# Weight products whose moving columns are read, and whose bank columns are written, from last to first

## The reference

```
h = rmsnorm(x); proj = h @ w_in          # 2048 x (512 + 4*768 + 12 + 2*768)
mixed = concat(pool_mixer, gated_deltanet, rglru_mixer)
x = x + mixed @ w_out                    # 2048 x 2048
x = x + (gelu(dwconv(gate)) * val) @ w_down   # gate, val = split(rmsnorm(x) @ w_up), 2 x 6144 wide
x = rmsnorm(x)
```

```
u = rmsnorm(x) @ w_in_2                  # 2048 x D_IN: latents, heads of three branches, gates
o_a, o_b, o_c = latent, difference and banded attention (8 heads each)
y = sum over n: sigmoid(gate_n) * ((o_n * silu(z_n)) @ w_branch[n])
x = x + y @ w_out_2
```

## Time and profile before

| | |
|---|---|
| median of three runs | 3365.55 us (3365.45 to 3366.45) |
| span of the profiled execution, first to last instruction | 3364.8 us |
| matmuls, of which in L191 to L193 and L205 to L207 | 27834, 24384 |
| busy: TensorE, VectorE, ScalarE, GpSimd | 3322.3, 2191.7, 1711.6, 309.8 us |
| HBM | 580 MB read, 173 GB/s over the span |

### The profile page before, as it was taken

How to read it: one execution, slowest core, us unless ns; L and a number is a source line. 1 busy time by engine, 2 the same in 40 slices (tenths; PEclk the granted TensorE clock), 3 DMA queues, 4 the chain that set the end, 5 groups by cost and what they waited for, 6 DMA issues and landing times. The chain is left out here.

```text
span 3364.8 us, 72970 instructions
## 1 busy us (share of the span) xinstructions
PE 3322.3 (99%) x27834; PEld 3282.9 (98%) x27834; DVE 2191.7 (65%) x3584; ACT 1711.6 (51%) x2803; POOL 309.8 (9%) x314
## 2 busy tenths in 40 slices
PE   8999999999999999999999999999999999999999
PEld 7999999999999998899999999999899999999999
DVE  7667666656656666678755665665778755666655
ACT  5555644434434455656544554444665654554443
POOL 1010100000000025011002200001012101210000
PEclk9999999999999999999999999999999999999999
DMA  5234555555555554444455545555444455445554
GB/s 190 107 112 148 176 186 189 189 186 187 188 187 187 187 187 159 139 163 158 161 197 184 183 161 188 188 201 177 146 153 163 156 178 209 172 162 188 187 206 162
DMA packets 90629, 584.28 MB, mean 174 GB/s; under 512 B 10480, under 2 KB 11120, under 8 KB 28400
## 3 DMA queue, kind: packets, MB, share of 16 engines
q1 hardware_dynamic: 88992, 577.47, 48.7%
q0 software_dynamic: 1488, 4.72, 0.4%
HBM read 580.05 MB, written 2.10 MB: 173 GB/s over the span
## 5 line engine op out<-in xcount | busy, mean ns | idle before, releaser
L172 DVE TENSOR_TENSOR w_lo<-raw,w_hi 128x768 fp32r<-128x768 f32 (+5 forms) x1202 | 1378.5, 1159 | 372.6 <-ACT w_hi L161 365.6
L191 PE MATMUL bank<-h,w_hi 128*128 128x256 f32 x5168 | 1459.3, 282 | 16.5 <-DVE w_lo L172 12.0
L161 ACT ACTIVATE w_hi<-raw 128x768 fp32r<-128x768 f32 (+4 forms) x1190 | 1095.7, 968 | 692.3 <-PE bank L193 615.4
L193 PE MATMUL bank<-h,w_lo 128*128 128x256 f32 x5168 | 1444.1, 279 | 0.0
L192 PE MATMUL bank<-h,w_hi 128*128 128x256 f32 x5168 | 1443.6, 279 | 0.0
L191 PEld LDWEIGHTS bank<-h,w_hi 128*128 128x128 f32 x5168 | 973.1, 188 | 22.0 <-DVE w_lo L172 10.2
L192 PEld LDWEIGHTS bank<-h,w_hi 128*128 128x128 f32 x5168 | 973.2, 188 | 2.6 <-issue 1.9
L193 PEld LDWEIGHTS bank<-h,w_lo 128*128 128x128 f32 x5168 | 972.8, 188 | 0.0
L191 PE MATMUL bank<-mixed,w_hi 128*128 128x256 f32 x2272 | 634.9, 279 | 0.7 <-DVE w_lo L172 0.7
L193 PE MATMUL bank<-mixed,w_lo 128*128 128x256 f32 x2272 | 634.5, 279 | 0.0
L192 PE MATMUL bank<-mixed,w_hi 128*128 128x256 f32 x2272 | 633.8, 279 | 0.0
(11 more groups left out here) (408 smaller groups left out, 3340.4 us busy)
## 6 DMA issues: line engine op xcount, KB each, us to landing
raw<-in_w SPq DMA_DIRECT2D x485, 1024.0 KB, 4.8
raw<-in_w_br SPq DMA_DIRECT2D x96, 512.0 KB, 3.8
raw<-in_w_uq SPq DMA_DIRECT2D x8, 768.0 KB, 4.4
raw<-in_w_ukv SPq DMA_DIRECT2D x8, 512.0 KB, 3.3
bias_t<-in_bias POOLq DMA_DIRECT2D x16, 192.0 KB, 4.2
x<-in_x SPq DMA_DIRECT2D x4, 512.0 KB, 7.7
raw<-in_w_kr SPq DMA_DIRECT2D x4, 512.0 KB, 3.3
out_x<-x SPq DMA_DIRECT2D x3, 512.0 KB, 7.5
```

What stands on the lines that cost most here:

```text
L161: act.activation(w_hi[:, b % 2, c], raw[:, b, c], ACT.Copy).then_inc(S["hi_done"], 1)
L172: dve.tensor_tensor(w_lo[:, b % 2, c], raw[:, b, c], w_hi[:, b % 2, c].bitcast(F32), ALU.subtract).then_inc(S["lo_done"], 1)
L191: pe.matmul(o, w_hi[:, b % 2, c], a_hi, start=start and k == t0, stop=False)
L193: last = pe.matmul(o, w_lo[:, b % 2, c], a_hi, start=False, stop=stop and k == t0 + nt - 1)
```

## The change

The three matmuls of each tile get the moving operand and the output as views whose columns run backwards. Both are reversed, so the result of each column lands in the column where it was. The stationary tiles, the readers of the banks and all other matmuls stay as they are.

```diff
+        def back(v):
+
+            return v[:, ::-1]
+
         def unit(pe, n, b, act_of, outs, ready=None):
...
-                    pe.matmul(o, w_hi[:, b % 2, c], a_hi, start=start and k == t0, stop=False)
-                    pe.matmul(o, w_hi[:, b % 2, c], a_lo, start=False, stop=False)
-                    last = pe.matmul(o, w_lo[:, b % 2, c], a_hi, start=False, stop=stop and k == t0 + nt - 1)
+                    pe.matmul(back(o), w_hi[:, b % 2, c], back(a_hi), start=start and k == t0, stop=False)
+                    pe.matmul(back(o), w_hi[:, b % 2, c], back(a_lo), start=False, stop=False)
+                    last = pe.matmul(back(o), w_lo[:, b % 2, c], back(a_hi), start=False, stop=stop and k == t0 + nt - 1)
...
         def unit_tiles(pe, n, b, act_of, o, k0, k1, ready=None):
...
-                pe.matmul(o, w_hi[:, b % 2, c], a_hi, start=k == 0, stop=False)
-                pe.matmul(o, w_hi[:, b % 2, c], a_lo, start=False, stop=False)
-                last = pe.matmul(o, w_lo[:, b % 2, c], a_hi, start=False, stop=k == KT - 1)
+                pe.matmul(back(o), w_hi[:, b % 2, c], back(a_hi), start=k == 0, stop=False)
+                pe.matmul(back(o), w_hi[:, b % 2, c], back(a_lo), start=False, stop=False)
+                last = pe.matmul(back(o), w_lo[:, b % 2, c], back(a_hi), start=False, stop=k == KT - 1)
```

## The result

The changed kernel takes 3388.89 us (median of four runs, 3388.36 to 3389.54) against 3366.0 us: a ratio of 1.0065, 95% interval 1.0053 to 1.0076. It is slower by 23 us. The forecast was no change, 3365.5 us; it was missed by 23.4 us, and the size lies far under the rival of half the rate.

What follows compares the result with a forecast made beforehand. TensorE was taken to bound the kernel by its 116.7 ns step. The profiled 3364.8 us plus 24384 x 0 gave 3364.8; with the timed runs' median 0.75 us higher, the forecast was 3365.5 us, range 3355 to 5770 us.

Steps and rivals of the forecast that it cites:

- the rival of half the rate: On the six edited matmul lines, downward columns take twice the time: 5763 us, up to 6128; chance 0.24.
- What bounds the kernel: TensorE bounds the kernel from end to end, through its step of 116.7 ns from matmul start to matmul start.
- The count of what is touched: Six edited calls, L191 to L193 and L205 to L207, make 24384 of the 27834 matmuls, 2846 us of 3364.8.
- The parts at no cost: Weight loads, accumulation order, waits, DMA queues and the forward bank reads of VectorE and ScalarE stay unchanged: no cost.
- Between these I take nought: Price of the downward walk on the edited matmuls, taken as zero between bounds of -163 us and +2397 to +2763 us.
- 24384 x 0: The sum's term for the downward walk: no added time on each of the 24384 edited matmuls, 3364.8 us kept.
- something in the stream, some 10 ns: Excess of TensorE's forward step over the 106.7 ns the clock allows, which another order could in principle change.
- The bound from below: Weight loads follow each other no closer than about 110 ns, so a quicker walk could save at most 163 us.
- A: On the edited matmuls, each downward column takes its own access, half rate: 5763 us, up to 6128; chance 0.24.
- B: Smaller price on the edited matmuls, start-up or some columns: one cycle each +10 us, 160 ns step +1056 us; chance 0.13.
- C: Faster: the edited matmuls' 10 ns of excess shrink to the loads' floor, -163 us, 3202 us; chance 0.05.
- D: The view is turned back on its way to the chip, nothing reversed: no change in time, inside the forecast's 0.58.

Runs made afterwards that it cites:

- f_w_later16: Against the kernel before, all reads forward: activation buffers declared ahead of the split weights, 64 unused bytes between them in place of 32; 3341.35 us, ratio 0.9924.

## Why the prediction was wrong, point by point

**What bounds the kernel: right.** TensorE from end to end, by its step of 116.7 ns. All 23 us went into that step, and none were hidden or came from a wait.

**The count of what is touched: right**, 24384 matmuls; the untouched ones kept their time.

**The parts at no cost: right** for the weight loads' count, the waits, the queues, the evacuations, and for the writes to the bank, which one experiment measured alone at +0.2 us.

**The step that failed** is the one after "Between these I take nought": "A stream that is set by a rate of columns, whatever they are, has no reason to care for the sign of the step." The step of 116.7 ns was not set by a rate of columns. Its 10 ns above 256 / 2.4 = 106.7 ns moved with the distance between two buffers: to 13.3 ns without the 32 bytes, and the forward kernel's time by -26 to +73 us with nothing changed but where its buffers lie. The term "24384 x 0" measured 24384 x 0.95 ns. An explanation would be that the sign of the walk changes where the read stands while the weights beside it are loaded, and so the same excess; that is argued, and what happens there in the memory stays open. The prediction had this excess in hand, called it "something in the stream, some 10 ns, that another order could in principle change", and used it only as a bound for a gain. The same sentence bounds a loss: a term whose cause isn't known can go both ways when the addresses change. The evidence taken against it was weaker than it looked. That the step is the same beside busy and idle engines is so, but the earlier trace rows can't show it, as their second window mixes in other matmuls (1188.79 us and 9927 matmuls are 119.8 ns each). It excludes the other engines as the cause; it says nothing on TensorE's own second stream, which runs beside every matmul. And L2610 and L2611, "at the same 0.12 us", were read at 10 ns of resolution. Averaged over their starts, the matmuls with swapped roles step 118.3 ns where the others step 116.8, both forward and with 256 columns. The trace of the kernel before thus held the warning: same columns, other operands, another step.

**The bound from below: the row doesn't bear its reason.** Two passes of 128 columns of plain float32 take 110 ns each at, by the prediction's own reading, two cycles a column; that is 256 cycles, 106.7 ns, so the columns can set this step as well as the loads. The 64-column passes at the same 110 ns are the better evidence for a floor by the loads. The fastest rhythm seen here, 340 ns a tile or 113.3 a matmul, stays above it.

**The rivals.** A (half rate, at least +2397 us) fell with the first result. B (a smaller price) had the right sign with a chance of 0.13; its one-cycle case gave +10 us, measured were +23, 2.3 cycles each. Its mechanism, a cost of the backward read as such, fell: the alternating kernel has half its reads backward and costs nothing, and without the 32 bytes backward is the faster direction. C (the excess shrinks) had the right term and the wrong direction for this change; f_w_later16 realised 26 of its 163 us. D fell: the view does reach the chip, since the reads alone change the time.

**The range** held the measured time, from 3355 to 5770 us, only because it reached to rival A; the span that mattered, 3359 to 3372 us for the likeliest case, missed it by 17 us.

## What to carry to other kernels

When a dense stream of matmuls steps above what columns and clock give (here 116.7 against 106.7 ns), ask what its reads meet before asking what order they have: move the moving operand against the stationary one by 32 and 64 bytes and read the count of matmuls in a full window. In this kernel edits that changed only addresses or the order of reads, with the same work, moved that excess either way, by up to 73 us; so compare such edits at more than one placement before saying what the edit itself costs.

## What the runs showed of the hardware that was not expected

- TensorE's step for 256 fp32r columns, each with its load of 128 x 128, depends on the distance in bytes between the moving operand and the stationary one in SBUF: forward, 120.0 ns without the unused bytes, 116.7 with 32, 117.8 with 64. With the two groups of buffers exchanged it is 118.4 with 32 bytes, and 114.2 to 117.6 within one kernel with 64. That it is the distance was shown by moving both by 32 bytes together, which kept the step of 120.0. That it is a meeting of the two reads, and where in the memory, was only argued. At what distance the pattern repeats wasn't tried.
- The average step took few values. Over twenty kernels the window of 400 us held 3332 to 3333, 3379 to 3380, 3395 to 3396, 3409, 3423 to 3428 or 3445 matmuls, and at one place a single execution changes between 340 and 353 ns for three matmuls.
- Reading the moving columns downward has no fixed price: between -37 and +50 us over the forward twin on this kernel, by the placement. Going down in runs of two or four columns costs what going down by single columns does (+21.6, +20.8, +22.9 us at the one place tried).
- Writing the bank's columns downward is free: +0.2 us on 24384 matmuls.
- The effect isn't additive over matmuls: a third of the reads backward costs +20.0 us, every second one -1.3 us.
